# Second output projection and embedding gate: seven block products per pair of feature blocks in place of eight

## The chip, the cores and the metric

One core of a Trainium2 chip. The metric is the device time of one execution in microseconds, the median of some runs. Everything is float32; matmuls take each operand as a high part (rounded to the type that TensorE multiplies fast) and a low part, the rest.

## What is computed

Two blocks of a network on 512 tokens of width 2048. The change is in the end of the second one (weights 2048 x 2048 each for `w_out` and `w_ple_gate`):

```
merged = g_a * (o_a @ w_up_a) + g_b * (o_b @ w_up_b)
x = x + merged @ w_out
x = x + sigmoid(x @ w_ple_gate) * (p @ w_ple)
return rms_norm(x, final_g)
```

`g_a`, `g_b` are sigmoids of logits made earlier in the block.

## The kernel before

Activations lie transposed: 16 tiles of 128 features x 512 tokens. A weight matrix comes as chunks of 128 x 1024 floats (512 KB), each holding eight 128 x 128 blocks: half of the input features (k) for one block of 128 output features. `plan` (line 93) lists all chunks in the order of use; SyncE's queue loads them into four slots `raw` (`load`, issued at line 2888). For each chunk ScalarE writes the high half `whi` (`halves`, line 1284), GpSimd the low half `wlo` (line 2761) by subtraction. There are three buffers for these pairs (`PAIR`), so the high half of a chunk waits until TensorE has used the chunk three places before it.

`feature_block` (line 577 ff., products in `three`) runs 8 k-blocks x 3 matmuls of 512 columns (high x high, high x low, low x high); two chunks, so 48 matmuls, make a block of 128 output features in one PSUM bank. `project` and `led` (the first two blocks side by side) go over the 16 blocks of a projection.

The merge (`MERGE`, line 89) is 32 such chunks of `w_up_a` and `w_up_b`; VectorE multiplies each result by 1 + tanh (line 2684) and adds the two branches into `MG` (line 2689). Then the activations `MG` are split: ScalarE writes `hhi` (line 1295) scaled by 0.5, VectorE `hlo` (`merged_lower`, line 2666), eight tiles before the last products, eight after. The output projection `wout2` follows; VectorE adds the earlier activations (line 2699) into `X2`, which is split in the same way (lines 1295, 1908). The gate projection `pleg` follows: ScalarE takes tanh from PSUM, VectorE gates (`gated`, lines 2707 and 2711), ScalarE squares, GpSimd adds the squares (line 2848).

The last two blocks of the gate, 14 and 15, run in token halves of 256 columns, so that the norm of the first half is ready earlier: `last_sum` sums over features, ScalarE takes the root, VectorE the reciprocal, `last_spread` transposes, and VectorE (line 2728) and GpSimd (line 2855) write the outputs. Every engine runs its own queue in program order and waits on semaphores; a bank is claimed again (`claim`) once what it held is read.

## Time and profile before

| | us |
|---|---|
| median of 3 runs | 2408.61 (2407.76 to 2409.06) |
| span of the profiled execution | 2407.4 |
| TensorE matmul busy | 2385.2 (99%) |
| TensorE weight loads busy | 1900.5 (79%), 188 ns each |
| GpSimd busy | 970.5 (40%) |
| VectorE busy | 923.2 (38%) |
| ScalarE busy | 859.8 (36%) |
| DMA | 308 MB, mean 128 GB/s |

The view of waits says who stood for whom, the groups by line and shape give the duration of one operation, the timeline the starts. The durations that a matmul shows are longer than the spacing of their starts, since they are pipelined; spacing is what counts. Times in a row are from the start of the span.

### The profile page before, as it was taken

How to read it: one execution, taken by the hardware profiler on the slowest of the kernel's cores; microseconds unless marked ns; L12 is line 12 of the kernel's file. 1: busy time of each engine (PE TensorE's matmuls, PEld its weight loads, DVE VectorE, ACT ScalarE, POOL GpSimd, SP SyncE). 2: the span in 40 equal slices, each digit the busy share in tenths (PEclk: the TensorE clock that was granted, in tenths of full speed). 3: DMA queues.
4: the chain of work that ended last, by engine and by line, in shares of the span. 5: the costliest groups of instructions: out<-in, count | busy, mean ns of one | idle time of the engine just before them, and what ended most of it. 6: DMA issues, size and time to landing. Idle time of an engine off the chain costs nothing.

```text
span 2407.4 us, 28505 instructions
## 1 busy us (share of the span) xinstructions
PE 2385.2 (99%) x11184; PEld 1900.5 (79%) x11184; DVE 923.2 (38%) x1519; ACT 859.8 (36%) x1331; POOL 970.5 (40%) x432
## 2 busy tenths in 40 slices
PE   9999999999999999999999999999999999999997
PEld 5676777778888888887788787878788888888887
DVE  7756366675301700403455443434321413203113
ACT  6455454542323422323343333333333213113322
POOL 2043333344555344443333242434344444444554
PEclk9999999999999999999999999999999999999999
DMA  9952333345443443332222232323333544453232
GB/s 376 399 209 62 122 110 111 112 145 171 156 141 127 147 131 90 97 101 82 79 62 88 71 109 88 110 88 102 96 94 103 166 142 131 129 172 117 90 105 88
DMA packets 100441, 307.96 MB, mean 128 GB/s; under 512 B 10577, under 2 KB 16209, under 8 KB 100305
## 3 DMA queue, kind: packets, MB, share of 16 engines
q1 hardware_dynamic: 100306, 306.13, 39.5%
q8 instruction: 89, 1.46, 0.2%
q14 instruction: 46, 0.38, 0.0%
HBM read 284.06 MB, written 20.97 MB: 127 GB/s over the span
## 4 chain that ended last, share of the span: by engine, by line
PE 87%; DVE 4%; issue 3%; POOL 2%; ACT 2%; DMA 1%; SPq 1%; POOLq 0%; DVEq 0%; ACTq 0%
PE bank L577 24%; PE bank L580 23%; PE bank L578 23%; PE bank L573 2%; PE bank L576 2%; PE bank L574 2%; POOL wlo L2761 2%; PE bank L1114 2%; PE bank L1138 2%; PE bank L1126 1%; DVE hlo L1908 1%; PE bank L894 1%; PE bank L905 1%; DMA rawx<-in_wst 1%; DVE hlo L2666 1%
## 5 line engine op out<-in xcount | busy, mean ns | idle before, releaser
L2761 POOL TENSOR_TENSOR wlo<-raw,whi 128x1024 fp32r<-128x1024 f32 x359 | 884.5, 2470 | 1161.9 <-ACT whi L1284 1161.9
L577 PE MATMUL bank<-hhi,whi 128*128 128x512 f32 (+1 forms) x2768 | 1083.6, 391 | 2.1 <-DVE hlo L1908 1.2
L580 PE MATMUL bank<-hhi,wlo 128*128 128x512 f32 (+1 forms) x2768 | 1073.3, 388 | 1.1 <-POOL wlo L2761 1.0
L578 PE MATMUL bank<-hlo,whi 128*128 128x512 f32 (+1 forms) x2768 | 1072.3, 387 | 0.0
L577 PEld LDWEIGHTS bank<-hhi,whi 128*128 128x128 f32 x2768 | 520.5, 188 | 123.6 <-issue 18.2
L580 PEld LDWEIGHTS bank<-hhi,wlo 128*128 128x128 f32 x2768 | 520.5, 188 | 110.8 <-POOL wlo L2761 4.1
L578 PEld LDWEIGHTS bank<-hlo,whi 128*128 128x128 f32 x2768 | 520.8, 188 | 103.0 <-issue 0.7
L1284 ACT ACTIVATE whi<-raw 128x1024 fp32r<-128x1024 f32 x365 | 384.3, 1055 | 583.6 <-PE bank L580 471.3
L2542 DVE TENSOR_SCALAR S<-S,sm 128x512 f32<-128x512 f32 (+1 forms) x64 | 78.0, 1219 | 0.6
L1749 ACT ACTIVATE S<-S,sm 128x512 f32<-128x512 f32 (+1 forms) x64 | 35.3, 551 | 117.3 <-DVE sm L2532 117.3
L576 PE MATMUL bank<-wlo,hhi 128*128 128x512 f32 x192 | 74.8, 390 | 1.7 <-POOL wlo L2761 1.7
L573 PE MATMUL bank<-whi,hhi 128*128 128x512 f32 x192 | 74.9, 390 | 0.2 <-ACT whi L1284 0.2
L574 PE MATMUL bank<-whi,hlo 128*128 128x512 f32 x192 | 74.8, 389 | 0.0
L2542 DVE TENSOR_SCALAR S2b<-S2b,sm 128x512 f32<-128x512 f32 (+1 forms) x64 | 73.5, 1149 | 0.0
L2388 DVE SCALAR_TENSOR_TENSOR X<-bank,sm,axr 128x512 f32<-128x512 f32 x16 | 12.0, 750 | 137.6 <-PE bank L580 137.6
L2699 DVE TENSOR_TENSOR X<-bank,axr 128x512 f32<-128x512 f32 x16 | 11.0, 690 | 138.4 <-PE bank L580 138.4
L2526 DVE CUSTOM_DVE_ANT_0 S<-bank,BT 128x512 f32<-128x512 f32 (+1 forms) x64 | 31.1, 486 | 85.4 <-PE bank L1114 85.4
L2707 DVE SCALAR_TENSOR_TENSOR tgt<-tgt,MG 128x512 f32<-128x512 f32 (+1 forms) x18 | 12.0, 669 | 131.1 <-ACT tgt L1859 122.2
L2558 DVE COPY PT<-bank 128x384 f32<-128x384 f32 (+2 forms) x48 | 20.0, 416 | 96.8 <-PE bank L1126 96.8
L1822 ACT ACTIVATE TS<-bank 128x512 f32<-128x512 f32 x32 | 18.9, 591 | 99.8 <-PE bank L580 94.5
L2788 POOL TENSOR_TENSOR sqa<-sqa,sqa 128x512 f32<-128x512 f32 x4 | 5.6, 1405 | 112.1 <-ACT sqa L1425 112.1
L576 PEld LDWEIGHTS bank<-wlo,hhi 128*128 128x128 f32 x192 | 36.0, 188 | 9.6 <-POOL wlo L2761 2.1
(339 smaller groups left out, 2177.7 us busy)
## 6 DMA issues: line engine op xcount, KB each, us to landing
raw<-in_wst SPq DMA_DIRECT2D x397, 512.0 KB, 3.6
rawx<-in_wst SPq DMA_DIRECT2D x54, 512.0 KB, 10.1
rawy<-in_wst SPq DMA_DIRECT2D x26, 512.0 KB, 4.7
tgs<-TS SPq DMA_DIRECT2D x32, 256.0 KB, 3.9
axr<-tgs SPq DMA_DIRECT2D x32, 256.0 KB, 4.0
X<-in_xt SPq DMA_DIRECT2D x4, 1024.0 KB, 12.9
axr<-in_xt SPq DMA_DIRECT2D x16, 256.0 KB, 2.8
x1s<-X SPq DMA_DIRECT2D x16, 256.0 KB, 2.0
```

What stands on the lines that cost most here:

```text
L573: e.matmul(o, xh, hi, start=first, stop=False)
L574: e.matmul(o, xl, hi, start=False, stop=False)
L576: return e.matmul(o, xh, lo, start=False, stop=last)
L577: e.matmul(o, hi, xh, start=first, stop=False)
L578: e.matmul(o, hi, xl, start=False, stop=False)
L580: return e.matmul(o, lo, xh, start=False, stop=last)
L1114: e.matmul(bks[n][0][:, off:off + wd], qq[pb:pb + 64, P * i:P * (i + 1)], kk[pb:pb + 64, 0:wd], start=True, stop=True).then_inc(*up("score ...
L1138: e.matmul(oo[64 * gb:64 * gb + 64, P * j:NT], vv, pt_piece(gb, j), start=False, stop=br == 1 and j == 3).then_inc(*up("pv_pe", "pv", u, g ...
L1284: e.activation(hi_of(c), slots[slot(c)], ACT.Copy).then_inc(*up("whi_act", "whi", c))
L1749: e.activation(sl, sl, ACT.Exp, scale=SM2, bias=smx[:, 8 + k:9 + k], accum_out=smx[:, 16 + k:17 + k]).then_inc(*up("exp_act", "exp", u, gb ...
L2542: e.tensor_scalar(sl, sl, ri[:, 4 * gb + i:4 * gb + i + 1], None, ALU.mult, ALU.bypass).then_inc(*up("soft_dve", "soft", u, gb, i))
L2761: e.tensor_tensor(lo_of(c), slots[slot(c)], hi_of(c).bitcast(F), ALU.subtract).then_inc(*up("wlo_pool", "wlo", c))
```

## The change

For a pair of output blocks the weights are four quadrants (a11, a12 and a21, a22: block one or two, first or second half of k) and the activations are four quadrants of 8 tiles x 256 tokens. Strassen's scheme in Winograd's form makes the pair from seven products of 8 k-blocks x 3 matmuls with 256 columns: a11 b11, a12 b21, s1 t1, s2 t2, s3 t3, s4 b22, a22 t4, where t1 to t4 are differences of activations and s1 to s4 sums of weights. All products of the eight pairs of `wout2` and of `pleg` run in this way. VectorE forms s1 to s4 in PSUM (`SA`, `SB`, two banks each) and their low halves; ScalarE and GpSimd do the other weights as before, and the differences and all splits of activations are shared out between the engines by hand. Per product VectorE adds 256 columns from PSUM to what is there (in the gate three of them are copied by ScalarE). `(1 + tanh) / 2` is now made by ScalarE ahead of VectorE's product. The four quadrants of a pair are loaded in the order a11, a21, a22, a12. The embedding comes back from DRAM block by block. In the last pair the second token half is ended first.

```diff
-MERGE = [(n, br, ("upa", "upb")[br]) for n, br in [(0, 1), (1, 1), (0, 0), (1, 0)]
+MERGED = [m for k in range(8) for m in (k, k + 8)]
+MERGE = [(MERGED[n], br, ("upa", "upb")[br]) for n, br in [(0, 1), (1, 1), (0, 0), (1, 0)]
...
+PAIRED = ("wout2", "pleg")
+PARTS = ("a11", "s1", "a12", "s2", "s4", "s3", "a22")
+LAST_PARTS = ("a11", "s1", "s2", "s4", "s3", "a12", "a22")
+QUADRANTS = ("a11", "a21", "a22", "a12")
+OPERAND = {"a11": "b11", "s1": "t1", "a12": "b21", "s2": "t2", "s4": "b22", "s3": "t3", "a22": "t4"}
...
+def parts(name, p):
+    return LAST_PARTS if (name, p) == ("pleg", 7) else PARTS
...
+def blocks_of(name, p):
+    return (p, p + 8) if name == "wout2" else (2 * p, 2 * p + 1)
...
-    led("wout2")
-    led("pleg")
+    out.extend((name, p, part) for name in PAIRED for p in range(8) for part in parts(name, p))
...
+            def pair_product(name, p, part, st, between=None):
...
+                last = (name, p) == ("pleg", 7)
+                first = part in ("a11", "s1", "a12", "a22")
+                w.wait_ge(*done("whi", c))
+                if part == "a11":
+                    o, prior = claim(0, "px", name, p)
+                elif part == "s1":
+                    o, prior = claim(1, "py", name, p)
+                elif part == "a12":
+                    o, prior = claim(2, "pz", name, p)
+                elif part == "a22" and last:
+                    o, prior = claim(7, "pw", name, p)
+                elif part == "a22":
+                    o, prior = banks[2], [done("prod", name, p, "a12")]
+                elif part == "s2":
+                    o, prior = banks[0], [done("prod", name, p, "a11")]
+                elif part == "s4":
+                    o, prior = banks[1], [done("prod", name, p, "s1")]
+                else:
+                    o, prior = banks[0], [done("prod", name, p, "s2")]
+                for f in prior:
+                    w.wait_ge(*f)
+                xh, xl = OPS[OPERAND[part]]
+                o = o[:, 0:256]
...
+                    w.wait_ge(*done("slo", st, OPERAND[part], k))
+                    ws = slice(k * P, (k + 1) * P)
+                    e.matmul(o, hi[:, ws], xh[:, k, :], start=first and k == 0, stop=False,
+                             skip_group_check=not first)
...
+                        between(k)
...
+                    ws = slice(k * P, (k + 1) * P)
+                    m = e.matmul(o, lo[:, ws], xh[:, k, :], start=False, stop=k == 7, skip_group_check=not first)
+                    if between:
...
+            for p in range(8):
+                for part in parts("wout2", p):
+                    pair_product("wout2", p, part, "m")
...
+            for part in parts("pleg", 7):
+                pair_product("pleg", 7, part, "x2", in_last if part == "a22" else None)
...
+            for i in range(32):
+                use()
...
+                e.activation(AXM[i % 8][:, :], AXM[i % 8][:, :], ACT.Identity, scale=0.5, bias=halfc).then_inc(
+                    *up("term_act", "axm", i))
...
+                if i == 29:
+                    merged("t2", 0, 7)
+                elif i == 30:
+                    merged("t3", 0, 7)
+            merged("b11", 0, 8)
+            merged("t1", 0, 8)
...
+            for p in range(8):
+                for g in range(7):
+                    use()
+                    if p == 0:
+                        for o, a, b in {0: [("b21", 0, 7), ("b21", 7, 8), ("t2", 7, 8), ("t3", 7, 8)],
+                                        1: [("b22", 0, 8)], 3: [("t4", 0, 8)]}.get(g, ()):
+                            merged(o, a, b)
+                    elif p == 7:
+                        for o, a, b in {1: [("b11", 0, 7)], 2: [("t1", 0, 7)], 3: [("b21", 0, 7)],
+                                        4: [("b11", 7, 8), ("t2", 0, 7)], 5: [("b22", 0, 7)],
+                                        6: [("t3", 0, 7), ("t1", 7, 8)]}.get(g, ()):
+                            residual(o, a, b)
...
+            def gate_tanh(n):
+                w.wait_ge(*done("prod", "pleg", n // 2, "a22" if n % 2 else "s4"))
+                w.wait_ge(*done("prod", "pleg", n // 2, "a12"))
+                e.activation(tgt[n % 2][:, :], tgt[n % 2][:, :], ACT.Tanh, scale=0.5).then_inc(*up("tanh_act", "pg", n))
...
+            def weight_sum(name, p, part):
+                c = INDEX[name, p, part]
+                q = {s: slots[PLACE[name, p, s]] for s in QUADRANTS}
+                for s in {"s1": ("a21", "a22"), "s2": ("a11",), "s3": ("a11", "a21"), "s4": ("a12",)}[part]:
...
+                    e.tensor_tensor(SA[:, :], q["a21"], q["a22"], ALU.add).then_inc(
+                        *up("sum_dve", "sum", name, p, part))
+                elif part == "s2":
...
+                        *up("sum_dve", "sum", name, p, part))
...
+                    e.tensor_tensor(SA[:, :], q["a11"], q["a21"], ALU.subtract).then_inc(
+                        *up("sum_dve", "sum", name, p, part))
...
+                    e.tensor_tensor(SB[:, :], q["a12"], SB[:, :], ALU.subtract).then_inc(
+                        *up("sum_dve", "sum", name, p, part))
...
+            def sum_lo(name, p, part):
...
+                e.tensor_tensor(lo_of(c), raw_of(c), hi_of(c).bitcast(F), ALU.subtract).then_inc(
+                    *up("wlo_dve", "wlo", c))
...
-                w.wait_ge(f"ax{n % 8}", 96 + 16 * (n // 8 + 1))
-                w.wait_ge(*done("mg", 15))
-                e.tensor_tensor(sub(X2, n), bank("proj", "wout2", n)[:, :], AXR[n % 8][:, :], ALU.add).then_inc(
-                    *up("res_dve", "res", "wout2", n, frees=("proj", "wout2", n)))
-            for k in range(8, 16):
-                lower(k, sub(X2, k), "x2", [done("res", "wout2", k), done("proj", "wout2", 15)])
+                    e.tensor_tensor(sub(MG, n), sub(MG, n), m2t[j % 2][:, :], ALU.add).then_inc(*up("mg_dve", "mg", n))
+                if i == 27:
+                    diff("m", "t3", 0, 7)
+                    diff("m", "t1", 0, 7)
+                elif i == 28:
+                    diff("m", "t2", 0, 7)
+                    diff("m", "t4", 0, 7)
+                    weight_sum("wout2", 0, "s1")
+                elif i == 29:
+                    diff("m", "t1", 7, 8)
+                    weight_sum("wout2", 0, "s2")
+                    prep_lo("m", "t2", 0, 7)
+                elif i == 30:
+                    sum_lo("wout2", 0, "s1")
+                    prep_lo("m", "b11", 0, 8)
+                    prep_lo("m", "t1", 0, 8)
+            diff("m", "t2", 7, 8)
+            diff("m", "t3", 7, 8)
+            diff("m", "t4", 7, 8)
+            prep_lo("m", "b21", 0, 7)
+            prep_lo("m", "b21", 7, 8)
+            prep_lo("m", "t2", 7, 8)
+            prep_lo("m", "t3", 7, 8)
...
+            def residual(p, part):
...
+                    frees = (of, "wout2", p) if part in ("s4", "a22") or part == "s3" and s == 0 else None
+                    e.tensor_tensor(quarter(n, s), bank(of, "wout2", p)[:, 0:256], quarter(n, s), ALU.add).then_inc(
+                        *up("prod_dve", "prod", "wout2", p, part, frees=frees))
...
+            for p in range(8):
+                for g, part in enumerate(PARTS):
+                    residual(p, part)
+                    to = next_of("wout2", p)
+                    if g == 0:
+                        sum_lo("wout2", p, "s2")
+                        weight_sum("wout2", p, "s4")
+                    elif g == 1:
+                        sum_lo("wout2", p, "s4")
+                        if p == 7:
+                            prep_lo("x2", "b11", 0, 7)
+                    elif g == 2:
+                        if p == 0:
+                            weight_sum("wout2", 0, "s3")
+                        sum_lo("wout2", p, "s3")
+                        if p == 7:
+                            prep_lo("x2", "t1", 0, 7)
+                    elif g == 3:
+                        weight_sum(*to, "s1")
+                        if p == 0:
+                            prep_lo("m", "t4", 4, 8)
+                        elif p == 7:
+                            prep_lo("x2", "b21", 0, 7)
+                    elif g == 4:
+                        weight_sum(*to, "s2")
+                        if p == 7:
+                            prep_lo("x2", "b11", 7, 8)
+                    elif g == 5:
+                        diff("x2", "t1", p, p + 1)
+                        diff("x2", "t2", p, p + 1)
+                        diff("x2", "t3", p, p + 1)
+                        sum_lo(*to, "s1")
+                        if p == 7:
+                            prep_lo("x2", "t1", 7, 8)
+                            prep_lo("x2", "t2", 0, 7)
+                    else:
+                        diff("x2", "t4", p, p + 1)
+                        if p == 7:
+                            prep_lo("x2", "b21", 7, 8)
+                            prep_lo("x2", "t2", 7, 8)
+                        weight_sum(*to, "s3")
             def gated(g, x, m, n, *t):
 
                 w.wait_ge(*done("pg", n, *t))
-                w.wait_ge("plr", 64)
+                w.wait_ge(f"pl{n % 3}", 16 * (n // 3 + 1))
                 e.scalar_tensor_tensor(g, g, 1.0, m, ALU.add, ALU.mult).then_inc(*up("out_dve"))
...
+            sum_lo("pleg", 7, "s2")
+            weight_sum("pleg", 7, "s4")
+            whole_gated(13)
+            sum_lo("pleg", 7, "s4")
+            sum_lo("pleg", 7, "s3")
+            gate_product(7, "s4")
+            gate_product(7, "s3")
+            last_gated(14, 1)
+            last_gated(15, 1)
+            gate_product(7, "a12")
+            last_root(1)
+            gate_product(7, "a22")
+            outputs(1, range(POOLED, 7))
             last_gated(14, 0)
             last_gated(15, 0)
+            outputs(1, range(7, 10))
...
-            last_gated(14, 1)
-            outputs(0, range(7, 16))
-            last_gated(15, 1)
-            last_root(1)
-            outputs(1, range(POOLED, 16))
+            outputs(1, range(10, 16))
+            outputs(0, range(POOLED, 16))
...
+            for i in range(32):
+                use()
+                if i == 30:
+                    prep_lo("m", "t3", 0, 7)
+            for p in range(8):
+                for g in range(7):
+                    use()
+                    if p == 0 and g == 1:
+                        prep_lo("m", "b22", 0, 4)
+                        prep_lo("m", "b22", 4, 8)
+                    elif p == 0 and g == 3:
+                        prep_lo("m", "t4", 0, 4)
+                    elif p == 7 and g == 6:
+                        prep_lo("x2", "t3", 0, 7)
+            for p in range(8):
+                for g in range(7):
+                    use()
+                    if p == 0 and g == 0:
+                        prep_lo("x2", "b22", 4, 7)
+                        prep_lo("x2", "t3", 7, 8)
+                        prep_lo("x2", "t4", 0, 5)
+                        prep_lo("x2", "t4", 5, 8)
+                    elif p and g == 1:
+                        squares(2 * p - 2)
+                    elif p and g == 3:
...
+                second_done(w)
+                e.dma_start(sub(X2, n), x1s[n]).then_inc(*up(f"ax{n}" if n < 8 else f"bx{n - 8}", by=16))
+            load(LINDEX["wout2", 0, "a12"])
```

## Rows read from the trace of the kernel before

**Rows 1.** The page's first part: busy us, share of the span, instructions.

```profile
PE 2385.2 (99%) x11184; PEld 1900.5 (79%) x11184; DVE 923.2 (38%) x1519; ACT 859.8 (36%) x1331; POOL 970.5 (40%) x432
```

**Rows 2.** TensorE's waits, 1800 to 2408: waiter, releaser, us, times, longest.

```profile
PE bank L577 <- DVE hlo L1908: 0.9, 2, 0.6
PE bank L580 <- POOL wlo L2761: 0.5, 1, 0.5
PE bank L577 <- DVE hlo L2666: 0.3, 1, 0.3
```

**Rows 3.** Timeline of VectorE in the merge: start, duration, line, operation, idle before.

```profile
1903.31 0.69 DVE L2684 SCALAR_TENSOR_TENSOR MG<-axr,bank 128x512 f32<-128x512 f32 x1 [4.03 <-PE bank L580]
1914.19 0.69 DVE L2684 SCALAR_TENSOR_TENSOR MG<-axr,bank 128x512 f32<-128x512 f32 x1 [4.03 <-PE bank L580]
```

**Rows 4.** Timeline of TensorE at the 256-column blocks, first and last of 26.

```profile
2366.99 0.28 PE L577 MATMUL bank<-hhi,whi 128*128 128x256 f32 x1
...
2369.98 0.28 PE L578 MATMUL bank<-hlo,whi 128*128 128x256 f32 x1
```

**Rows 5.** Groups of instructions by shape, 1920 to 2408 (columns as the page's part 5).

```profile
L2761 POOL TENSOR_TENSOR wlo<-raw,whi 128x1024 fp32r<-128x1024 f32 x84 | 204.0, 2432 | 175.9 <-ACT whi L1284 175.9
L578 PEld LDWEIGHTS bank<-hlo,whi 128*128 128x128 f32 x719 | 135.3, 188 | 25.3
L1284 ACT ACTIVATE whi<-raw 128x1024 fp32r<-128x1024 f32 x84 | 88.6, 1058 | 251.7 <-PE bank L580 251.7
L2699 DVE TENSOR_TENSOR X<-bank,axr 128x512 f32<-128x512 f32 x16 | 11.0, 690 | 138.4 <-PE bank L580 138.4
L1295 ACT ACTIVATE hhi<-X 128x512 fp32r<-128x512 f32 x16 | 8.6, 616 | 1.0 <-DVE X L2699 1.0
L2728 DVE SCALAR_TENSOR_TENSOR MG<-X,vt,bank 128x256 f32<-128x256 f32 x22 | 8.9, 474 | 2.1 <-PE bank L1235 2.1
L2855 POOL TENSOR_TENSOR MG<-MG,rsc 128x256 f32<-128x256 f32 x10 | 7.4, 778 | 18.9 <-ACT rsc L1890 18.9
```

**Rows 6.** The same view of VectorE, whole span: two SBUF inputs, GpSimd resting.

```profile
L2071 DVE TENSOR_TENSOR wlo<-rawx,whi 128x1024 fp32r<-128x1024 f32 x10 | 12.2, 1222 | 3.1 <-ACT whi L1284 3.1
L1908 DVE TENSOR_TENSOR hlo<-unb,hhi 128x512 fp32r<-128x512 f32 x16 | 9.8, 681 | 4.3 <-ACT hhi L1295 4.3
```

**Rows 7.** Lines 2666 and 2761 within 2046 to 2048 (min/median/max); VectorE's timeline.

```profile
L2666 DVE SCALAR_TENSOR_TENSOR hlo<-MG,hhi x1: 2875/2875/2875, 2045.9 to 2045.9; 128x512 fp32r<-128x512 f32 x1
L2761 POOL TENSOR_TENSOR wlo<-raw,whi x1: 2957/2957/2957, 2045.3 to 2045.3; 128x1024 fp32r<-128x1024 f32 x1
...
2043.48 11.51 DVE L2666 SCALAR_TENSOR_TENSOR hlo<-MG,hhi 128x512 fp32r<-128x512 f32 x8
```

**Rows 8.** The page's sixth part: a chunk of weights, KB, us to landing.

```profile
raw<-in_wst SPq DMA_DIRECT2D x397, 512.0 KB, 3.6
```

**Rows 9.** Timeline at the end, some of its rows.

```profile
2392.46 0.28 PE L580 MATMUL bank<-hhi,wlo 128*128 128x256 f32 x1
...
2394.58 0.40 ACT L1881 ACTIVATE sqc<-X 128x256 f32<-128x256 f32 x1
...
2398.15 4.40 DVE L2728 SCALAR_TENSOR_TENSOR MG<-X,vt,bank 128x256 f32<-128x256 f32 x11 [0.73 <-PE bank L1235]
```

**Rows 10.** TensorE in windows: us, busy (instructions), granted clock, DMA share, GB/s.

```profile
2393.00:2394.00 1.00, 0.00 (x0) 1.00 1.03 353
...
2397.00:2398.00 1.00, 0.53 (x3) 0.79 0.00 0
2398.00:2399.00 1.00, 0.54 (x3) 0.50 0.00 0
```

587 lines of the change are left out of this document (426 added, 161 removed).

## Prediction

> **What bounds the kernel now.** I read the page first. TensorE is busy for 2385 of 2407 us and no other engine for more than 41% [rows 1], so the time is TensorE's queue, and a change counts for what it does to the spacing of the matmuls and to the gaps between them. The waits of TensorE over the last quarter name hardly 2 us ahead of the final sum, and I use three of them: 0.9 us and 0.3 us for the low halves of the activations, 0.5 us for a low half of weights [rows 2]. Next the spacing, since the change halves the columns of each matmul. In the merge VectorE takes up one result each 5.44 us, so two of them 10.88 us apart [rows 3]; that is 48 matmuls of 512 columns, 226.7 ns each. The last two blocks of the gate already run with 256 columns: from 2366.99 to 2369.98 the timeline has 26 of them back to back, 25 spacings, 119.6 ns each [rows 4]. Twice 119.6 is 239.2: half the columns cost 12.5 ns more per pair of matmuls, so not all of an eighth fewer columns arrives.
>
> The side engines come next, because the change loads them. On GpSimd one low half of a 128x1024 chunk takes 2.43 us; ScalarE's copy of it 1.06 us and of 512 columns 0.62 us; VectorE adds a PSUM block of 512 columns in 0.69 us and handles 256 in about 0.41 (0.474 is a mean with one outlier in it, eleven of them take 4.40 us at the end); GpSimd needs 0.78 us for 256 [rows 5]. VectorE with both inputs in SBUF takes 1.22 us for 1024 columns and 0.68 for 512 when GpSimd rests [rows 6]; a line through the two gives 0.41 for 256, 2.03 for 1792 and 2.30 for 2048. But when GpSimd works, the same 512-column operation took 2.88 us, while GpSimd's own took 2.96; eight of them, 5.4 us of work, took 11.51 us [rows 7]. Operations with one input in PSUM stayed at 0.69 us throughout [rows 3]. So an operation of VectorE with two SBUF inputs and one of GpSimd exclude each other, each for the whole of the other's instruction. Nothing waited for VectorE here, because it had hardly any work in these stages. A chunk of weights lands 3.6 us after its issue [rows 8].
>
> **The change part by part.** (1) *Matmuls.* Per pair of blocks 96 matmuls of 512 columns (21.76 us) become 7 products of 24 of 256 columns, 168 x 0.1196 = 20.09 us. Before, 30 blocks at 10.88 and 192 matmuls at 0.1196: 326.4 + 23.0 = 349.4 us. After, 16 x 20.09 = 321.5. Less: 27.9 us. The three gaps of 1.7 us are replaced by those below: 29.6 us off in all. The other order of the products (all high halves, then eight low ones) doesn't alter the count.
>
> At this place the Trainium skill, page "TensorE: Matmul & The Clock Gate", section "The mechanism" (packing small matmuls), says that a weight load overlaps with matmuls in flight only when its row group differs. The trace has 188 ns for each load [rows 5] beside a spacing of 119.6 [rows 4], so loads are covered here although all 128 rows are used. By that rule the sum would be far higher (a rival below); by the rows it stays.
>
> (2) *VectorE in the middle of the pairs.* Per pair in the output projection: 4 sums of weights and 4 low halves of them at 1.22, 8 evacuations and 4 differences at 0.41: 14.7 of 20.1 us. I laid its queue against a product of 2.87 us. A chunk's high half waits for the product three before it and takes 1.06; its low half then follows in 1.2 (VectorE) or 2.4 us (GpSimd) and is first read 1.9 us into its product, which gives 3 to 4 us of slack. Only two of the sums read SBUF twice; GpSimd's three low halves (7.3 us per pair) delay one of them by up to 2.2 us, inside that slack. In the gate VectorE has 9.8 + 5 x 0.41 + 4 x 0.69 = 14.6 us, and ScalarE 7.4 + 1.2 + 2.4. Cost: nothing; the cover is the three weight buffers, and gone it would cost what is late per pair (a rival). DMA carries as many chunks as before, four per pair; each slot's new chunk is asked for at least 8 us before its use.
>
> (3) *First preparation, merge to projection.* Before, 16 low halves stood beside the last products. Now VectorE has, from the end of product 27 of the merge (t = 0; four more products of 5.44 us follow, to 21.8) until the low half of b11 is there: merging 4.2, differences t3, t1, t2, t4 at 2.03 and one of 0.41, two sums 2.4, low halves of t2 2.03, of the first sum 1.22, of b11 2.30. Together 20.7 us, nearly the whole 21.8. GpSimd works in the same time: three low halves of weights and 4.05 us for t3, and each that starts while VectorE is at a PSUM operation shuts out the next one: 2.4 + 1.7 + 1.7 + 4.05 = 9.9 us. So b11 is ready at 30.7, and TensorE stands 8.9 us. Behind it in VectorE's queue are t1, the last merge, three differences and b21, until 39.3, where the third product should start at 36.4: 2.9. Then b22 and t4 are split by ScalarE and GpSimd one after the other (2 x 2.4 each) while sums, low halves and the fifth to seventh products wait for them in turn: 0.4 + 2.3 + 1.9 more. Sum 16.4 us. With no exclusion the same walk gives 4; I take 16.4, since rows 7 show it for these very operations.
>
> (4) *Second preparation, projection to gate.* In the last pair VectorE's 14.7 us get 8.1 us of low halves (b11, t1, b21, t2) and 1.6 of single tiles: 24.4 in 20.1. GpSimd's low halves of a22 and of the next a11 and a12, and t3 (4.05), shut it out for 2.0 + 2.4 + 2.4 + 3.5 = 10.3. The evacuation of the last product, which should be at 20.5, comes at 36, and it frees the bank of the third product of the gate, due at 25.8. Then ScalarE, which waited for that evacuation with b21, t2, b22, t3, t4 (3.5 us) ahead of the high half of s2, lets the fourth product start at 41.3 (due 28.7); the later ones catch up little: 13.6 us. Without exclusion 3. I take 13.6.
>
> (5) *End.* From the last gate matmul (2392.7) the trace has a tanh, a sum, the root and eleven outputs of the second half, to 2402.6, then DMA [rows 9]. Added ahead of the tanh: one PSUM addition, 0.41. VectorE's queue has six outputs of the other half (6 x 0.40) behind the last reciprocal, where 0.7 us were spent waiting, so the eleven begin 2.1 us later (lower bound 0 if the DMAs at the end hide it, upper bound all six and the stand of TensorE in a22 for the first sum, 3.5). Sum 2.5.
>
> (6) *Clock.* TensorE's granted clock is 1.00 up to 2397, when it had stood from 2392.7 but for sixteen short matmuls; it is 0.79, then 0.50 of the 2.4 GHz level behind that [rows 10]. A stand of 8.9 us could bring it to 1.2 GHz. Before shows no return; bounds 0 and 2.9 (one product of 24 at half speed). I take 0, since the stand is at the edge of what the rows show before the fall (4.3 us with sixteen short matmuls in it), and keep 2.9 for the range.
>
> (7) *Merge.* ScalarE gets 32 activations of 0.6 us with (1+x)/2, ahead of VectorE's product; it has 1.1 of 5.44 us of work there. The first tile's loading now holds ScalarE for some 4 us, under a VectorE burst that already lasts longer. Zero, 1 at most.
>
> Sum, against the profiled execution: 2407.4 - 29.6 + 16.4 + 13.6 + 2.5 = 2410.3. The median of the runs is 2408.6, 1.2 above that span: 2411.5.
>
> **The rivals.** *Cheap transitions (faster).* The bursts slide past each other: then 4 + 3 + 2.5 replace 32.5, 2407.4 - 29.6 + 9.5 + 1.2 = 2388.5. For it: exclusion decides only where both engines want to start together, and 5.2 of VectorE's 20.7 us are PSUM work and need no turn. Against it: 20.7 of 21.8 us is full without any. A mixture, half the exclusion, gives 2400.
> *VectorE falls behind in every pair (slower).* Place: sums s1 and s3, differences and gate updates against GpSimd's 7.3 to 9.9 us per pair. It decides from 5.4 us of exclusion per pair (20.1 - 14.7); if all of 7.3 hit, 1.9 us more in each of 14 pairs, + 27: 2438. Against it, the walk in (2) found 2.2.
> *Spacing grows in a long run.* From 129.5 ns (21.76/168) nothing is left of (1); 125 would give + 14.5: 2426. Only 192 such matmuls are in the trace, all at 119.6 to 120.
> *Weight loads uncovered.* 107 ns of added columns' time (226.7 - 119.6) plus 188: 295 ns, + 471 us: 2883. It is the rule of the skill's TensorE page above; a spacing below the load's own 188 ns speaks against it.
>
> **How the numbers follow.** Forecast 0.50, with its own range 2401 to 2420 (each preparation 3 to 5 us either way; end 0 to 3.5; clock up to 2.9); of it 0.12 lies below 2403.8, 0.28 within, 0.10 above 2413.4. Cheap or half-priced transitions 0.28: 0.23 faster, 0.05 same. VectorE behind 0.14, spacing 0.07, loads 0.01: all slower. A comparison here can tell about 0.2%, 4.8 us. So faster 0.35, same 0.33, slower 0.32. The range 2389 to 2430 leaves out the lower end of the cheap case and what is above 2430.
>
> **What would show it.** Spacing in the middle of the pairs 119.6 ns and 20.1 us from one a11 to the next. TensorE's waits: the first product of the projection for a VectorE low half, near 9 us; the third and fourth products of the gate for a VectorE evacuation and a ScalarE copy, near 10 us. VectorE operations with two SBUF inputs at 3 to 6 us beside GpSimd's. The prediction is wrong if those waits sum to under 20 or over 40 us, if a pair in the middle takes over 20.5 us, or if the clock row falls.

## The result and the profile after

| | before | after |
|---|---|---|
| median | 2408.19 us (2407.70 to 2409.06, 4 runs) | 2426.78 us (2425.47 to 2427.55, 4 runs) |
| span of the profiled execution | 2407.4 | 2424.6 |

The changed kernel is 0.77% slower: ratio 1.0077, 95% interval 1.0063 to 1.0092. TensorE is busy 16.3 us less and the time grows by 18.6 us.

The page's first part of after, against [rows 1]:

```profile
PE 2368.9 (98%) x12240; PEld 1939.1 (80%) x12240; DVE 1148.0 (47%) x1762; ACT 942.7 (39%) x1427; POOL 979.5 (40%) x425
```

TensorE is still 98% busy, VectorE has 225 us more. TensorE's waits from 1800 to 2425 (waiter, releaser, us in total, times, longest), against [rows 2]:

```profile
PE bank L1324 <- DVE hlo L2928: 10.4, 4, 7.4
PE bank L1354 <- ACT sqc L2095: 7.6, 2, 5.5
PE bank L1324 <- DVE T4L L2928: 5.3, 1, 5.3
PE bank L1324 <- DVE X L3040: 4.7, 3, 3.0
PE bank L1324 <- ACT whi L1395: 4.0, 2, 2.1
PE bank L1324 <- issue: 3.6, 1, 3.6
PE bank L1365 <- DVE rbc L3115: 0.9, 1, 0.9
PE bank L1332 <- DVE wlo L2976: 0.7, 1, 0.7
```

L1324 is the first matmul of a product, L1332 its low weights, L1354 the final sum, L2928 VectorE's low halves of activations, L3040 its evacuations. Each wait has a place, which TensorE's timeline gives (start, duration, line, operation, idle before):

```profile
2043.51 0.55 PE L1324 MATMUL bank<-hhi,whi 128*128 128x256 f32 x1 [7.38 <-DVE hlo L2928]
...
2071.25 0.58 PE L1324 MATMUL bank<-T4H,whi 128*128 128x256 f32 x1 [5.25 <-DVE T4L L2928]
...
2220.30 0.36 PE L1324 MATMUL bank<-hhi,whi 128*128 128x256 f32 x1 [3.57 <-issue]
...
2230.90 0.55 PE L1324 MATMUL bank<-hhi,whi 128*128 128x256 f32 x1 [3.03 <-DVE X L3040]
...
2283.65 0.38 PE L1324 MATMUL bank<-hhi,whi 128*128 128x256 f32 x1 [1.89 <-ACT whi L1395]
...
2306.66 0.39 PE L1324 MATMUL bank<-hhi,whi 128*128 128x256 f32 x1 [2.08 <-ACT whi L1395]
...
2408.77 0.55 PE L1354 MATMUL bank<-ct,ssc 128*128 128x1 f32 x2 [5.47 <-ACT sqc L2095]
```

The first two stand in the first pair of the projection, the next two at the start of the gate, the next two in the gate's third and fourth pair, the last behind the last product.

A ledger makes the kernels comparable. In an undisturbed pair the seven products start 2.88 us apart: 20.16 us. I take the end of the merge, 16 pairs of 20.16, and what each stretch has above that; the last column is what follows the nominal end of the last pair. The sum of a row is its span to 0.1.

| kernel | span | merge ends | first preparation (pairs 0, 1) | second (last pair, gate's first) | other gate pairs | behind |
|---|---|---|---|---|---|---|
| after | 2424.6 | 2036.1 | 18.7 | 13.7 | 6.5 | 27.1 |
| x1_no_exclusion | 2406.2 | 2037.9 | 9.4 | 2.5 | 7.3 | 26.6 |
| x2_early_diff | 2420.2 | 2037.7 | 15.5 | 13.7 | 3.6 | 27.1 |
| x3_tail_order | 2420.9 | 2038.0 | 18.9 | 13.7 | 3.6 | 24.1 |
| x4_scale_later | 2418.2 | 2035.9 | 19.1 | 13.7 | 0.0 | 27.0 |
| y1_m_order | 2419.4 | 2038.1 | 13.2 | 15.1 | 3.5 | 26.8 |
| y2_x_order | 2424.5 | 2036.4 | 18.5 | 15.4 | 4.6 | 27.0 |
| y3_all | 2413.7 | 2039.8 | 13.1 | 14.6 | 0.0 | 23.5 |
| z1_no_excl_others | 2392.5 | 2036.3 | 7.0 | 2.5 | 0.0 | 24.1 |
| w1_busy | 2409.8 | 2038.6 | 11.9 | 13.3 | 0.0 | 23.4 |
| v1_on_vector | 2408.7 | 2036.8 | 9.7 | 11.7 | 4.3 | 23.6 |
| v2_whole_busy | 2407.8 | 2037.4 | 8.3 | 10.0 | 4.2 | 25.2 |

Pairs 2 to 6 of the projection have 0.0 in every row. The merge ends between 2035.9 and 2039.8 although hardly anything ahead of it differs: single spans can't be compared closer than that. The stretches can, but not equally well: kernels with the same code in a stretch differ by up to 0.6 us in the first preparation, 0.8 in the second and 0.7 behind (v2_whole_busy apart), while the other gate pairs have 3.5 to 7.3 in the six kernels that leave them alone.

### The profile page after: what moved, and what is told of

The parts are those of the page before. It is cut to its first block, busy times and chain, and to the rows that moved or that the text cites. A ratio compares the mean times of both kernels' runs of the same rounds, so it can differ in the third digit from the quotient of the medians.

```text
span 2424.6 us, 31158 instructions
## 1 busy us (share of the span) xinstructions
PE 2368.9 (98%) x12240; PEld 1939.1 (80%) x12240; DVE 1148.0 (47%) x1762; ACT 942.7 (39%) x1427; POOL 979.5 (40%) x425
## 4 chain that ended last, share of the span: by engine, by line
PE 87%; DVE 6%; ACT 2%; issue 2%; DMA 1%; SPq 1%; POOL 0%; DVEq 0%; ACTq 0%; POOLq 0%
PE bank L664 20%; PE bank L667 20%; PE bank L665 20%; PE bank L1332 3%; PE bank L1324 3%; PE bank L1326 3%; PE bank L660 2%; PE bank L661 2%; PE bank L663 2%; PE bank L1201 2%; PE bank L1225 2%; PE bank L1213 1%; DVE hlo L2122 1%; PE bank L981 1%; PE bank L992 1%
## 5 line engine op out<-in xcount | busy, mean ns | idle before, releaser
L3216 POOL TENSOR_TENSOR wlo<-raw,whi 128x1024 fp32r<-128x1024 f32 x295 | 730.9, 2484 | 1039.9 <-ACT whi L1408 1015.7
L664 PE MATMUL bank<-hhi,whi 128*128 128x512 f32 x2224 | 877.5, 395 | 1.2 <-DVE hlo L2122 0.6
L667 PE MATMUL bank<-hhi,wlo 128*128 128x512 f32 x2224 | 867.5, 390 | 0.6 <-POOL wlo L3216 0.5
L665 PE MATMUL bank<-hlo,whi 128*128 128x512 f32 x2224 | 866.6, 390 | 0.0
L667 PEld LDWEIGHTS bank<-hhi,wlo 128*128 128x128 f32 x2224 | 417.8, 188 | 90.7 <-POOL wlo L3216 3.4
L1408 ACT ACTIVATE whi<-raw 128x1024 fp32r<-128x1024 f32 x301 | 317.0, 1054 | 396.5 <-PE bank L667 287.4
L3205 POOL TENSOR_TENSOR wlo<-raw,whi 128x1024 fp32r<-128x1024 f32 x48 | 135.9, 2840 | 133.3 <-ACT whi L1395 133.3
L1324 PE MATMUL bank<-hhi,whi 128*128 128x256 f32 x512 | 130.3, 290 | 21.3 <-DVE hlo L2928 10.4
L1326 PE MATMUL bank<-hlo,whi 128*128 128x256 f32 x512 | 129.4, 289 | 0.0
L1324 PEld LDWEIGHTS bank<-hhi,whi 128*128 128x128 f32 x512 | 101.2, 198 | 23.1 <-issue 17.2
L1395 ACT ACTIVATE whi<-bank 128x1024 fp32r<-128x1024 f32 x64 | 65.3, 1023 | 87.9 <-PE bank L1332 34.6
L2976 DVE TENSOR_TENSOR wlo<-bank,whi 128x1024 fp32r<-128x1024 f32 x64 | 78.1, 1221 | 36.9 <-ACT whi L1395 36.7
```

Of the source, the lines that this page charges most:

```text
L664: e.matmul(o, hi, xh, start=first, stop=False)
L665: e.matmul(o, hi, xl, start=False, stop=False)
L667: return e.matmul(o, lo, xh, start=False, stop=last)
L1324: e.matmul(o, hi[:, ws], xh[:, k, :], start=first and k == 0, stop=False, skip_group_check=not first)
L1326: e.matmul(o, hi[:, ws], xl[:, k, :], start=False, stop=False, skip_group_check=not first)
L1408: e.activation(hi_of(c), slots[slot(c)], ACT.Copy).then_inc(*up("whi_act", "whi", c))
```

## The experiments

The first four change one thing of the changed kernel each. Totals of kernels without an interval are single executions.

**Exclusion taken away.** The second input comes from PSUM; the work and its duration stay. These operands are wrong, so the kernel leaves out a part of the computation and only its time counts.

```diff
-                e.tensor_tensor(OPS[o][1][:, a:b, :], source(st, o, a, b), OPS[o][0][:, a:b, :].bitcast(F),
+                e.tensor_tensor(OPS[o][1][:, a:b, :], source(st, o, a, b),
+                                banks[7][:, 0:256].unsqueeze(1).to_broadcast([P, b - a, 256]),
...
+                two = banks[7][:, 0:256].unsqueeze(1).to_broadcast([P, b - a, 256])
                 e.tensor_tensor(source(st, o, a, b), one_, two, ALU.subtract).then_inc(
```

> In the two preparations each difference and each low half that VectorE makes of activations takes its second input from a bank of PSUM instead of SBUF: the same operations, sizes, places in the queue and waits, but only one SBUF input. The low halves and differences of the activations are therefore wrong; nothing else is left out. Weight sums s1, s3 and the gate updates keep their two SBUF inputs. Theory (exclusion between VectorE and GpSimd): the first preparation's loss (18.6 us in the changed kernel, clock included) falls to 5 to 9, the second's (13.7) to 4 to 6, the span from 2424.6 to 2400 to 2406. Rival (the amount of work in VectorE's queue and the order of the waits): the same queue takes the same time, 2422 to 2425.

Measured 2407.9 us. The first preparation falls from 18.7 to 9.4 (a little above the 5 to 9 expected), the second from 13.7 to 2.5 (below the 4 to 6). The same two operations in VectorE's timeline, first of after:

```profile
2022.53 3.62 DVE L2913 TENSOR_TENSOR TM<-MG 128x1792 f32<-128x1792 f32 x1
...
2032.20 4.16 DVE L2913 TENSOR_TENSOR MG<-MG 128x256 f32<-128x256 f32 x1
```

GpSimd's timeline of after has beside the second:

```profile
2031.57 4.51 POOL L3300 TENSOR_TENSOR T3L<-TM,T3H 128x1792 fp32r<-128x1792 f32 x1
```

VectorE's timeline of this kernel:

```profile
2017.60 2.02 DVE L2914 TENSOR_TENSOR TM<-MG,bank 128x1792 f32<-128x1792 f32 x1
...
2028.76 0.42 DVE L2914 TENSOR_TENSOR MG<-MG,bank 128x256 f32<-128x256 f32 x1
```

One tile took 4.16 us beside a 4.51 us operation of GpSimd and 0.42 without the exclusion. So 20.5 us of the transitions go with the exclusion and not with VectorE's load (the falls of TensorE's clock behind the stands are in this sum); it is the largest cause. The updates of the gate keep both inputs in SBUF here, and its other pairs lose 7.3 us, as much as before or more. The Trainium skill, page "SBUF — State Buffer", section "SBUF: two separate sides", says the pair of ports that VectorE and GpSimd share is an exclusive lock for the whole instruction; this trace agrees, with 4.16 against 0.42 us.

**Differences made earlier.** They are made tile by tile through the merge.

```diff
-                if i == 27:
-                    diff("m", "t3", 0, 7)
-                    diff("m", "t1", 0, 7)
+                if i % 4 == 3 and i < 28:
+                    for o in ("t3", "t1", "t2", "t4"):
+                        diff("m", o, i // 4, i // 4 + 1)
                 elif i == 28:
-                    diff("m", "t2", 0, 7)
-                    diff("m", "t4", 0, 7)
```

> The differences t1 to t4 for the first preparation are made tile by tile as soon as a pair of merged tiles is there, all through the merge, instead of in four operations of 1792 columns after products 27 and 28. Theory (VectorE's burst ahead of b11 is too long for the four products it has): 8.1 us of work and two exclusions leave the burst, the stand of TensorE at the first product falls from 7.4 us to under 1.5 and with it the fall of the clock; span 2412 to 2417. Rival (what follows, b21, b22 and t4, sets the start of the later products in any case): under 3 us are gained, 2421 or more.

Measured 2421.9. The first stand fell from 7.38 to 3.01 us, but the preparation only from 18.7 to 15.5. Some 8 us of VectorE's work were taken out of the burst; what stayed grew. VectorE's low halves of t2 and of b11 and t1, which took 2.01 and 4.48 us in after, in the timeline of this kernel:

```profile
2031.87 4.75 DVE L2928 TENSOR_TENSOR T2L<-TM,T2H 128x1792 fp32r<-128x1792 f32 x1
...
2038.27 6.66 DVE L2928 TENSOR_TENSOR hlo<-MG,hhi 128x2048 fp32r<-128x2048 f32 x2
```

GpSimd's work hadn't moved, and VectorE's next operations met it instead. The total is the rival's; 2.9 of the 4.8 us gained came in the gate, which the edit doesn't touch. The wait for t4 stayed at 5.2 us. Its chain in VectorE's timeline of after:

```profile
2066.11 1.81 DVE L2950 TENSOR_TENSOR bank<-raw 128x1024 f32<-128x1024 f32 x1 [4.33 <-DMA raw<-in_wst]
2067.84 3.36 DVE L2928 TENSOR_TENSOR T4L<-TM,T4H 128x1024 fp32r<-128x1024 f32 x1
```

VectorE stood 4.33 us for the weights of the next pair, with t4's low half queued behind. SyncE issued these loads only when the late sum s3 of the first pair had read the slots, as its timeline shows:

```profile
2059.23 8.00 SPq L3388 DMA_DIRECT2D raw<-in_wst  x4
```

That is a dependence of the queue's order; y1_m_order below changes it.

**Both tanh ahead of the squares in the last pair**, so that the second doesn't stand behind a square that waits for VectorE.

```diff
                     g = half_of(tgt[n % 2], t)
                     e.activation(g, g, ACT.Tanh, scale=0.5).then_inc(*up("tanh_act", "pg", n, t))
-                    if n == 15:
-                        w.wait_ge(*now("root_act"))
-                        e.activation(spare, epsc, ACT.Sqrt).then_inc(*up("root_act"))
+                w.wait_ge(*now("root_act"))
+                e.activation(spare, epsc, ACT.Sqrt).then_inc(*up("root_act"))
+                for n in (14, 15):
```

> ScalarE takes both tanh of a token half before the two squares, in place of tanh, square, tanh, square, with the table load behind both. Theory (at the end the second tanh stands behind a square that waits for VectorE): the end is 2.5 to 4 us shorter, span 2420.5 to 2422. Rival (the seventeen outputs in VectorE's queue and the DMA behind them, or the clock, set the end): under 1 us.

Measured 2422.6: the stretch behind fell from 27.1 to 24.1, the waits for the squares from 2.08 and 5.47 to 0.74 and 4.37. ScalarE's timeline of after shows what was taken away:

```profile
2402.63 0.41 ACT L2089 ACTIVATE tgt<-tgt 128x256 f32<-128x256 f32 x1
2406.08 0.42 ACT L2095 ACTIVATE sqc<-X 128x256 f32<-128x256 f32 x1 [3.04 <-DVE X L3099]
2406.40 0.40 ACT L2089 ACTIVATE tgt<-tgt 128x256 f32<-128x256 f32 x1
```

The gate's fourth pair lost 0 here instead of 3.9, and in x2_early_diff and y1_m_order only one of the two stood as well: these stands come or stay away with the phase of the engines. What decides it shows in the next experiment.

**The scaling by the final gain moved** from the gate's second to fourth pairs to its fourth to eighth.

```diff
-                if n < POOLED:
-                    w.wait_ge(*done("x3sq", n))
-                    e.activation(sub(X2, n), sub(X2, n), ACT.Identity, scale=V("final_g", n)).then_inc(
-                        *up("out_act", "x3g", n))
...
+                    if g == 3 and p >= 3:
+                        scaled(p - 3)
```

> The scaling of tiles 0 to 4 by the final gain, 0.72 us each on ScalarE, is moved from pairs 1 to 3 of the gate to pairs 3 to 7, one a pair. Theory (in pairs 2 and 3 ScalarE's queue runs late by these operations and brings the high half of s4 late, 6.5 us of stands): 4 to 6.5 us gained, span 2418 to 2421. Rival (the exclusion of gate updates by GpSimd's low half of a12 is what brings it late, whoever else is in the queue): under 1.5 us.

Measured 2419.9; the gate's pairs fell from 6.5 to 0.0 (from 3.5 to 7.3, if all kernels with the earlier scaling are counted). ScalarE's timeline of after, in the gate's third pair:

```profile
2275.20 0.63 ACT L2051 ACTIVATE tgt<-tgt 128x512 f32<-128x512 f32 x1 [3.80 <-DVE tgt L3143]
2275.74 0.61 ACT L2062 ACTIVATE sqc<-X 128x512 f32<-128x512 f32 x1
2276.39 0.72 ACT L2065 ACTIVATE X<-X,vt 128x512 f32<-128x512 f32 x1
2277.02 0.36 ACT L2046 ACTIVATE tgt<-bank 128x256 f32<-128x256 f32 x1
2277.28 1.01 ACT L1395 ACTIVATE whi<-bank 128x1024 fp32r<-128x1024 f32 x1
...
2282.30 0.38 ACT L2046 ACTIVATE tgt<-bank 128x256 f32<-128x256 f32 x1 [4.00 <-DVE X L3099]
2282.58 1.02 ACT L1395 ACTIVATE whi<-bank 128x1024 fp32r<-128x1024 f32 x1
```

The high half of s2 queues behind four others, VectorE stands for it, the gating behind VectorE is late, and the next copy of ScalarE waits for the gating, with the high half of s4 behind. ScalarE is 39% busy: the order in its queue costs.

It isn't the whole cause. What lengthened the 3.80 us wait above is a gate update of VectorE, with both inputs in SBUF, beside GpSimd's low half of a12. VectorE and GpSimd in the timeline of after:

```profile
2272.06 2.77 DVE L3099 SCALAR_TENSOR_TENSOR X<-tgt,X 128x512 f32<-128x512 f32 x1
...
2271.48 2.81 POOL L3205 TENSOR_TENSOR wlo<-raw,whi 128x1024 fp32r<-128x1024 f32 x1 [1.62 <-ACT whi L1395]
```

The update alone takes 0.69. In the gate's second to seventh pairs of the twelve kernels, 72 pairs, 18 lose time, and exactly these 18 have an update of 2.77 to 2.81 us; it is at most 1.08 in the others. With a scaling ahead in ScalarE's queue such a pair loses 2.0 to 3.9 us, without it 1.1 to 1.6. So the rival named the trigger and the theory what makes it dear: moving the scaling brought VectorE's updates ahead of GpSimd's operation. No run takes the exclusion alone out of these updates.

**Order round the first preparation** (on top of the early differences).

```diff
-                if i == 29:
+                if i == 28:
                     merged("t2", 0, 7)
-                elif i == 30:
+                elif i == 29:
                     merged("t3", 0, 7)
...
                 elif i == 28:
+                    prep_lo("m", "t2", 0, 7)
                     weight_sum("wout2", 0, "s1")
...
                         sum_lo("wout2", p, "s4")
+                        if p == 0:
+                            weight_sum("wout2", 0, "s3")
...
                         if p == 0:
                             prep_lo("m", "t4", 4, 8)
+                        weight_sum(*to, "s1")
```

> Only the order of the side engines' work round the first preparation is changed: the differences t1 to t4 are made tile by tile through the merge, the halves of t2 and t3 stand one product earlier on each engine, the low half of t2 stands ahead of the first sum of weights, the first pair's sum s3 stands one product earlier, and the low half of t4 stands ahead of the next pair's sum s1, which waits for a DMA. Theory (what remains of the first preparation after the early differences is a matter of queue order): the fifth product's stand of 5.2 us falls below 2, the first stand of 3.0 with early differences stays under 3, the loss in the first preparation falls from 18.6 to 6 to 10 us, total 2415 to 2419. Rival (the bursts only slide into each other, since VectorE's and GpSimd's work of the stage is the same in sum and excludes itself as before): the loss stays at 14 or more, total 2421 to 2424.

Measured 2421.2. The wait for t4 fell from 5.2 to 0.62 us, as expected; the first stand was 4.50 instead of under 3, since GpSimd's t3, a product earlier, now shuts out a merge addition and a difference (3.83 and 2.50 us), and the second pair stood 2.09 for an evacuation. The preparation lost 13.2: a little under the rival's 14, far from the 6 to 10 of the theory. The total is the rival's.

**Order in the second preparation.**

```diff
                         weight_sum(*to, "s1")
-                        elif p == 7:
-                            prep_lo("x2", "b21", 0, 7)
...
                             prep_lo("x2", "t1", 7, 8)
-                            prep_lo("x2", "t2", 0, 7)
+                            prep_lo("x2", "b21", 0, 7)
...
                             prep_lo("x2", "b21", 7, 8)
+                            prep_lo("x2", "t2", 0, 7)
```

> Only VectorE's order in the last pair of the projection is changed: the low half of b21 stands two products later and that of t2 one product later, so that the evacuations and differences of the last pair come before them. Theory (the second preparation's 13.7 us are the late evacuation of the last products, which queue behind low halves that are needed only later): 3 to 6 us less, total 2421 to 2424. Rival (VectorE is simply full in this pair, and what is moved back makes the third or fourth product of the gate late instead): within 2 us of 2426.8.

Measured 2426.2, the rival: the gate's first product now waits 0.19 instead of 3.57 us, and the low half of t2, moved back, took 5.09 us for two operations beside GpSimd and made the fourth product late, which also waited 3.3 us for the low half of its weights, queued behind. 15.4 instead of 13.7.

**All orders together.**

> The edits of the two kernels before it in this set, with the final scaling later in the gate (worth 6.9 us alone) and both tanh ahead of the squares in the last pair (worth 3.7 us alone in net). No arithmetic is changed. If the parts add: 2426.8 - 9 (first preparation) - 4 (second) - 6.5 - 4 = 2403, range 2399 to 2409, about level with or a little below the kernel before (2408). If the bursts only slide: 2411 to 2416, still slower than before.

Measured 2412.7 in ten runs, ratio to before 1.0019 (1.0010 to 1.0029). The end and the gate's pairs add as expected (23.5 and 0.0), the two preparations still lose 13.1 and 14.6: the bursts only slid.

**No exclusion, scaling and tanh moved:** the edits of x1_no_exclusion, x4_scale_later and x3_tail_order in one kernel.

> VectorE's low halves and differences of activations take their second input from a PSUM bank (so these operands hold wrong numbers, and the results too), and the final scaling is later in the gate and both tanh come ahead of the squares in the last pair. If the three causes are separate and add: 2407.9 (no exclusion alone) - 6 (scaling) - 3.5 (end) = 2398 to 2400, 0.4% under the kernel before: what the seven products could bring when the transitions are free of exclusion. If they overlap: 2402 to 2406.

Measured 2394.2, lower than expected. The gate's pairs gave back 7.3, not 6, and the end 2.5; the merge ended 1.6 us earlier, and the first preparation lost 7.0 instead of 9.4 without an edit to it: with the same stand of 3.1 us the clock fell in x1_no_exclusion and not here. So the causes add, and the further 4 us don't come from the edits. In a kernel that doesn't compute the split, the seven products thus come to about 13 us under before.

**TensorE kept busy in its stands.**

```diff
+            def fill(name, p, part, k):
+                for i in range(FILL.get((name, p, part, k), 0)):
...
+                    e.matmul(banks[7][:, 0:P], C("ident"), C("ident"), start=True, stop=True)
```

> The kernel of y3_all with 87 spare products of the identity (128 columns, float32, into a bank that nobody reads) put where TensorE stands in the two preparations: 20 ahead of the first product of the projection, 10, 5 and 3 ahead of its third, sixth and seventh, 11 ahead of the second pair, 38 in the first pair of the gate; about 0.21 us each. They keep TensorE busy while it waits, so that its clock need not fall; nothing that it waits for is changed. In y3_all the products behind the stands lasted longer than 2.88 us by about 4 us in the first preparation and 5 in the second, at 0.5 to 0.8 granted. Theory (most of that is hidden, since the next low half is late anyway; only the last slow product of each preparation, 1.4 us each, moves what follows): 2 to 4 us less than y3_all's 2412.7, so 2409 to 2411. Rival (every slow product counts): 7 to 10 us less, 2403 to 2406. Second rival (spare matmuls don't hold the clock, or end late and delay the products themselves): 2413 or more.

Measured 2410.3, ratio 1.0009 (0.9999 to 1.0018), 2.4 us under y3_all. TensorE in windows (us, busy and instructions, granted clock, DMA share, GB/s), of y3_all:

```profile
2044.00:2052.00 8.00, 7.37 (x48) 0.79 0.01 2
...
2068.00:2076.00 8.00, 5.79 (x35) 0.79 0.40 131
...
2236.00:2244.00 8.00, 7.11 (x39) 0.62 0.60 229
```

and of this kernel:

```profile
2044.00:2052.00 8.00, 8.00 (x69) 1.00 0.00 0
...
2068.00:2076.00 8.00, 8.00 (x71) 1.00 0.43 135
...
2236.00:2244.00 8.00, 7.50 (x62) 1.00 0.57 207
```

The clock stayed up and each preparation gave back 1.2 to 1.3 us (13.1 to 11.9, 14.6 to 13.3), as the theory had it: a slow product in front of a late low half costs nothing, only the last one of a preparation moves what follows. That the clock is the cause rests on the medians of ten runs each, since 1.2 us in a stretch isn't far above what equal code varies by; how its price is shared out among the products is argued.

**GpSimd's activations given to VectorE.** In y3_all GpSimd takes these for the second preparation, beside weights:

```profile
2222.72 3.60 POOL L3301 TENSOR_TENSOR hlo<-X,hhi 128x768 fp32r<-128x768 f32 x1
...
2227.59 4.62 POOL L3301 TENSOR_TENSOR T4L<-TX,T4H 128x1280 fp32r<-128x1280 f32 x1 [0.39 <-ACT T4H L1975]
```

```diff
                     weight_sum("wout2", 0, "s2")
+                    prep_lo("m", "t3", 0, 7)
...
                         sum_lo("pleg", p, "s4")
+                        if p == 0:
+                            prep_lo("x2", "t3", 0, 7)
+                            prep_lo("x2", "t3", 7, 8)
```

> The kernel of y3_all, with GpSimd's low halves of activations beside the two preparations given to VectorE (t3 in the first; t3, t4 and b22 in the second), and VectorE's order in the second preparation laid out anew: the evacuation of the last product ahead of b21. GpSimd takes 15 us for its share in the second preparation and 5 in the first; VectorE would need 5.4 and 2.0 of its own. Theory (while the engines exclude each other, work given to the slower one costs VectorE more than doing it itself): first preparation 2 to 4 us less, second 3 to 6 less, together 2404 to 2408 against y3_all's 2412.7. Rival (the exclusion is only partial, so more work on VectorE makes it later): 2413 or more.

Measured 2409.4, ratio 1.0004 (0.9995 to 1.0014), above the expected 2404 to 2408 and below the rival. The first preparation fell from 13.1 to 9.7, the second from 14.6 to 11.7, though VectorE has more to do; 4.3 came back in the gate's pairs, where the high half of a sum is 1.0 to 1.3 us late three times. Each time a gate update has met GpSimd's low half, as in VectorE's timeline of the gate's third pair:

```profile
2263.38 2.77 DVE L3101 SCALAR_TENSOR_TENSOR X<-tgt,X 128x512 f32<-128x512 f32 x1
```

In y3_all every update of these pairs takes 0.69: the phase of the queues decides, and the scaling isn't ahead here. What is left of the exclusion shows in VectorE's timeline: GpSimd's two low halves of weights shut out t3, 2.35 us of work:

```profile
2225.78 6.74 DVE L2932 TENSOR_TENSOR T3L<-TX,T3H 128x1792 fp32r<-128x1792 f32 x2
```

**Whole operations, and TensorE kept busy.** The low halves of b21, t2, b22 and t3 in one operation each, and 52 spare products.

```diff
-                            prep_lo("x2", "t3", 0, 7)
-                            prep_lo("x2", "t3", 7, 8)
+                            prep_lo("x2", "t3", 0, 8)
```

> The kernel of v1_on_vector with two edits: in the second preparation VectorE makes the low halves of b21, t2, b22 and t3 in one operation each instead of two, so that GpSimd can shut it out once and not twice (in v1_on_vector the two operations for t3 took 6.74 us, 2.35 of them work, and the sixth product stood 2.51 for them), and 52 spare products of the identity stand in the waits, as in w1_busy. No arithmetic is changed. Theory (both are small and add): 2 us for t3, about 2 for the clock, together 2404 to 2407 against v1_on_vector's 2409.4: by 0.05 to 0.15% under the kernel before, too little to call. Rival (the time of the preparation is set by the chain of sums and halves, not by t3): 2408 to 2410.

Measured 2408.2, ratio 1.0000 (0.9991 to 1.0009). The total is the rival's. The preparations did fall by 1.4 and 1.7 us, but 1.6 of it went again in the last product, where the granted clock was 0.88 and 0.70 (1.00 in v1_on_vector) behind the same wait of 0.76 us. So orders, work moved to VectorE and spare products bring the change from 18.6 us over the kernel before to level with it; none of these kernels beats it by more than can be measured.

## Why the prediction was right or wrong

The forecast of 2411.5 was 15.3 us low; the measured 2426.8 lies in its range (2389 to 2430), and on the side of slower, to which it gave 0.32. The forecast's own range, 2401 to 2420, was missed; the wider one held because it makes room for rivals that didn't occur. Of the three signs of being wrong that it names, one stayed away (TensorE's waits ahead of the sums are 29 us, between 20 and 40) and two came: the clock fell, and two pairs in the gate took 22.8 and 24.1 us. Of its span of 2410.3 against 2424.6:

- (1) *Matmuls: right.* Products of 2.88 us, 120.0 ns for a matmul, 20.16 us a pair instead of 20.09: +1.1 in all. Nine of sixteen pairs have it exactly. The rivals of a growing spacing and of uncovered loads fell. The rule on loads in the Trainium skill, page "TensorE: Matmul & The Clock Gate", section "The mechanism", does not describe this kernel: the loads' mean is 198 ns beside a spacing of 120.
- (2) *VectorE in the middle of the pairs: right for pairs 2 to 6 of the projection, wrong for the gate.* Sums and low halves there take 1.22 us, as in [rows 6], and none loses anything:

```profile
L2950 DVE TENSOR_TENSOR bank<-raw 128x1024 f32<-128x1024 f32 x5 | 6.1, 1223 | 0.0
```

  That is the group of s1, two inputs in SBUF, in the pairs 2 to 6 (busy us, mean ns, idle before). In the gate 6.5 us came that the step had at nothing. It had a delay of up to 2.2 us by GpSimd, inside a slack of 3 to 4. The delay was 2.1 us, of a gate update, and wasn't inside the slack: it passes through ScalarE's queue to the high halves of s2 and s4. The step summed ScalarE's work to 11.0 us of 20.1 and left out the scaling (0.72), and it compared shares where the order of four operations ahead of a high half decided. That moving the scaling ends the loss is shown by x4_scale_later, the part of the collision by the traces alone.
- (3) *First preparation: the mechanism right, the size 2.3 low, two terms missed.* 16.4 expected, 18.7 measured; b11 was expected at t = 30.7, and was there at 29.1 (7.4 us of stand instead of 8.9). Without exclusion the walk gave 4, x1_no_exclusion 9.4. The walk didn't follow SyncE's queue: sum s3 late, so loads late, so t4 late. And it had no clock: the stands sum to 14.3 us, the rest is products at the lower clock. Exclusion as such was worth 9.3 us, not 12.4.
- (4) *Second preparation: the mechanism right, the agreement to 0.1 us luck.* 13.6 expected, 13.7 measured; without exclusion 3 expected, 2.5 measured. The gate's third product, held by the late evacuation, started 35.0 us after the first product of the projection's last pair (36 expected), the fourth at 40.0 (41.3). But the fourth waited for nothing; the third had run 5.00 us at the lower clock, which the step put at nothing, and 3.57 us stood at the gate's first product, for which the walk had nothing. The stands sum to 10.0 us. Its own walk ends at 41.3 - 28.7 = 12.6; the last 1.0 of the 13.6 is worked out from nothing.
- (5) *End: wrong in size.* From the last gate matmul to the end 21.3 us instead of 14.7 [rows 9]: +6.6, where 2.5 was taken and 3.5 was the upper bound; and the last pair itself lost about 3.5 more than the last blocks before, with the stand for the first sum and its clock. The step counted VectorE's additions and outputs and missed that ScalarE's second tanh stands behind a square which waits for VectorE, and that the second sum runs at a granted clock of 0.50 when the stand for it is over. VectorE then has 17 outputs where 11 took 4.40 us:

```profile
2412.19 6.74 DVE L3123 SCALAR_TENSOR_TENSOR X<-X,vt,bank 128x256 f32<-128x256 f32 x17
```

- (6) *Clock: wrong, 0 taken, 2.9 as bound.* It fell behind four stands in the preparations and the gate, of 7.4, 5.3, 3.0 and 2.1 us, and again in the last pair. The step had expected a stand of 8.9 us beside rows that show a fall after 4.3, so its own rows spoke against the 0. Its price in the two preparations was 2.5 us in y3_all, by w1_busy; after itself wasn't run with spare products.
- (7) *Merge: right.* It ended 3.2 us earlier in this execution and within 2035.9 to 2039.8 in all, against 2039.3 before; the difference is no larger than that between executions.

Sum of the misses: 1.1 + 2.3 + 0.1 + 6.5 + 7.6 (end and last pair) - 3.2 (merge) = 14.4, of the 14.3 that are to be explained.

Two rivals came nearer than the forecast for reasons that didn't occur: the growing spacing with 2426 (it stayed at 120.0 ns), and VectorE behind in every pair with 2438 (pairs 2 to 6 lose 0.0). What the prediction weighed too little is that each of its costs had an upper side that queue order could add to, and hardly a lower one: the sums of the two transitions held, and what was put at nothing or little (gate, end, clock) came out above it.

## What to carry to other kernels

When a change frees the bounding engine and loads others, cost the transitions and the end by walking each queue, with the DMA queue among them: 27 us of saved matmuls were lost in transitions, at the end and in one engine's queue, places that no mean of busy time shows. Between VectorE with two SBUF inputs and GpSimd, add the works instead of overlapping them, and move the work to the faster of the two when both want to run at once (3.4 and 2.9 us here); reordering alone mostly shifts the collision. An engine at 39% can still set the time, when an operation that nobody waits for stands ahead of one that TensorE waits for. And a collision of 2.1 us can cost nothing or 3.9, by the phase of the queues: look for it in every pair, not in the mean.

## What the runs showed of the hardware

Behind most of TensorE's stands of 3 to 7 us the granted clock was 0.57 to 0.81 in windows of 8 us, and products that take 2.88 us at 1.00 took up to 4.8 in after, 5.3 in x4_scale_later. It doesn't fall behind every such stand: the gate's first product waited 3.57 us in after and 3.58 in x4_scale_later. The window that holds it, first of after, then of x4_scale_later (columns as above):

```profile
2220.00:2228.00 8.00, 6.21 (x48) 1.00 0.07 11
...
2220.00:2228.00 8.00, 7.54 (x42) 0.62 0.05 9
```
 87 spare products in the stands held the clock at 1.00 in every window of the preparations, and brought 2.4 us.

VectorE's operations with one operand in PSUM ran at their own duration beside GpSimd in every run (2.02 us for 1792 columns, as against up to 4.75 with both in SBUF). What a collision costs VectorE isn't set by the size of its own operation: 0.41 us of work took 4.16.
